# Prompt tiles that store their mixed rows to DRAM, and a second phase that does out-projection, norm and router for all tiles with the decode chain between its steps

## The reference

```python
xn = rms_norm(x, norm1); proj = xn @ w_in          # q 512 | k 128 | v 128 | z 512 | xBC 1024 | dt 8
q, k = rope(rms_norm(q)), rope(rms_norm(k))
attn = sliding_window_attention(q, k, v, window=128, sinks)      # sample rows: 128 cached keys and values
ssm  = ssd(conv4(xBC), dt, a, chunk=128) ; g = ssm * silu(z) ; ssm = group_rms_norm(g) * ssm_norm
h = x + concat(attn, ssm) @ w_out
t = rms_norm(h, norm2)                             # router: best of 4 groups, best 2 of its 8 experts
y = h + sum_k gate_k * (silu(t @ w_gate[e_k]) * (t @ w_up[e_k])) @ w_down[e_k]      # 32 experts, FF 128
```

## Time and profile before

| | |
|---|---|
| median of 3 runs | 940.5 us (936.82 to 942.17) |
| profiled execution, first to last instruction | 939.0 us |
| TensorE busy | 823.0 us, 88% |
| VectorE busy | 479.8 us, 51% |
| ScalarE busy | 258.4 us, 28% |
| GpSimd busy | 147.8 us, 16% |
| mean granted TensorE clock | 0.923 |
| moved by DMA | 119.43 MB |

### The profile page before, as it was taken

How to read it: one execution, slowest core, us unless ns; L and a number is a source line. 1 busy time by engine, 2 the same in 40 slices (tenths; PEclk the granted TensorE clock), 3 DMA queues, 4 the chain that set the end, 5 groups by cost and what they waited for, 6 DMA issues and landing times.

```text
span 939.0 us, 13161 instructions
## 1 busy us (share of the span) xinstructions
PE 823.0 (88%) x4478; PEld 583.9 (62%) x4478; DVE 479.8 (51%) x1357; ACT 258.4 (28%) x607; POOL 147.8 (16%) x238
## 2 busy tenths in 40 slices
PE   5999999999999999999999995298599999999910
PEld 2877577676686695785786532243388887777800
DVE  1766585675765766766765731175412222222236
ACT  1251351431531621522513412141022222221200
POOL 0011001010101110110110110023133333333200
PEclk9999999999999999999999997557689999999965
DMA  7940100100100101001001001564589998887268
GB/s 254 313 119 2 68 1 2 69 1 1 69 0 23 46 0 59 10 0 69 0 0 50 8 18 62 164 253 134 184 276 332 338 331 292 315 292 289 81 227 335
DMA packets 56354, 119.43 MB, mean 127 GB/s; under 512 B 15198, under 2 KB 27246, under 8 KB 56286
## 3 DMA queue, kind: packets, MB, share of 16 engines
q1 hardware_dynamic: 43590, 89.31, 27.9%
q0 software_dynamic: 9216, 16.93, 4.9%
q10 hardware_dynamic: 3504, 12.68, 3.5%
...
## 4 chain that ended last, share of the span: by engine, by line
issue 46%; PE 21%; DMA 14%; SPq 7%; POOL 5%; DVE 3%; ACT 1%; POOLq 1%; DVEq 1%; ACTq 0%
DMA w_arena<-in_w_down 8%; PE bank L1689 8%; PE bank L1695 4%; SPq L408 3%; SPq L404 3%; POOL rstd L1273 3%; DMA w_arena<-y_dram 3%; PE bank L1405 3%; PE bank L1418 2%; DMA w_arena<-in_w_in 1%; DVE cv L891 1%; POOL xde L1304 1%; POOL xd L1301 1%; DMA pT<-v_new 1%; POOLq L1272 1%
## 5 line engine op out<-in xcount | busy, mean ns | idle before, releaser
L1418 PE MATMUL bank<-w_arena,xT 128*128 128x512 f32 (+3 forms) x464 | 174.8, 533 | 3.2 <-DMA w_arena<-in_w_in 3.2
L1418 PEld LDWEIGHTS bank<-w_arena,xT 128*128 128x128 f32 (+1 forms) x464 | 79.4, 175 | 88.7 <-issue 83.1
L1689 PEld LDWEIGHTS bank<-w_arena 128*128 128x128 f32 x992 | 116.9, 195 | 26.0 <-issue 20.6
L1689 PE MATMUL bank<-w_arena 128*128 128x128 f32 x992 | 119.1, 279 | 7.4 <-DMA w_arena<-in_w_down 6.4
L1435 PE MATMUL bank<-xT,w_arena 128*128 128x128 f32 x1024 | 116.8, 275 | 0.0
L1435 PEld LDWEIGHTS bank<-xT,w_arena 128*128 128x128 f32 x1024 | 116.1, 192 | 0.5
L1271 POOL TENSOR_TENSOR stat<-stat,eps 128x1 f32<-128x1 f32 (+4 forms) x35 | 6.8, 193 | 447.1 <-ACT junk L557 160.0
L1208 DVE TENSOR_TENSOR w_arena<-w_arena,bank 128x128 f32<-128x128 f32 x32 | 9.2, 288 | 112.8 <-ACT w_arena L692 112.8
L1695 PE MATMUL bank<-w_arena 128*128 128x512 f32 x124 | 60.4, 609 | 0.7 <-DVE w_arena L1208 0.7
L1449 PE MATMUL bank<-w_out_sb,aT 128*128 128x512 f32 x128 | 57.7, 593 | 0.0
L1449 PE MATMUL bank<-w_out_sb,gT 128*128 128x512 f32 x128 | 57.5, 592 | 0.0
...
## 6 DMA issues: line engine op xcount, KB each, us to landing
...
```

Source lines behind the costliest of these rows:

```text
L1418: ins = pe.matmul(out, xT[:, k, 0:n], w_in[:, k, cols], start=k == 0, stop=k == KC - 1)
L1689: ins = pe.matmul(out[:, a * P:(a + 1) * P], gu[:, a, k, :], xgT[w % 2][:, k, :], start=k == 0, stop=k == KC - 1)
```

## The change

The tile loop now ends at the SSD rows. Attention output and normed SSD rows of a tile share one buffer, `mix`, which the SP queue stores to `mix_dram` (`spill`). A second phase of nine steps follows, in the order tiles 0 to 6, sample rows, tile 7 (`ORDER`). Step i loads `mix` and x of its tile back (`load_back`, two buffers), multiplies in two halves of 512 columns (`pe_out(i, 0)`, `pe_out(i, 1)`), and between the halves and behind them come the transposes, ranks and router of the steps before and the pieces of the decode chain. `dve_front` is cut in three and its first two parts move ahead of the SSD gate; ACT's softplus moves with them. The new key and value row are issued ahead of the cache copies. The expert phase and the last part are as before, but the program asks for `dynamic_dma_scratch_size=8192`.

```diff
--- before.py
+++ after.py
...
+        mix_dram = nc.dram_tensor("mix_dram", (TILES, P, D), F32, kind="Internal").ap()
...
-        aT = sb("aT", [P, REP, P])
+        mix = sb("mix", [P, KC, P])
+        aT, gT = mix[:, 0:REP, :], mix[:, REP:KC, :]
+        mix_back = [sb(f"mix_back{u}", [P, KC, P]) for u in range(2)]
...
+        ORDER = (*range(TILES - 1), TILES, TILES - 1)
...
+        def back(i):
+            return x[(i + 1) % 2]
+
+        def back_landed(i):
+            return 32 * (i // 2) + (32 if ORDER[i] < TILES else 16)
...
+            def spill(tile, dst):
+                now(sp, "at gt", tile)
+                sp.dma_start(dst, mix[:, :, :].rearrange("p k n -> p (k n)")).then_inc(mix_out, 16)
...
                     sp.wait_ge(first_in, 32)
-                    sp.wait_ge(S["td"], t0 + (u + CREDIT + 1))
+                    sp.wait_ge(S["qkr"], t0 + (u + CREDIT + 1))
...
+                    sp.wait_ge(S["xn"], t0 + (u + CREDIT + 1))
                     sp.dma_start(x[u][:, :], flat_x[bass.ds(t0 * P + (u + 2) * P, P), :]).then_inc(x_in[u], 16)
...
+                    spill(t0 + u, mix_dram[bass.ds(t0 + u, 1)].rearrange("a p n -> (a p) n"))
...
+            def load_back(i):
+                tile = ORDER[i]
+                if tile < TILES:
+                    sp.dma_start(mix_back[i % 2][:, :, :].rearrange("p k n -> p (k n)"), mix_dram[tile]).then_inc(back_in[i % 2], 16)
+                    sp.dma_start(back(i)[:, :], flat_x[tile * P:(tile + 1) * P, :]).then_inc(back_in[i % 2], 16)
+                else:
+                    sp.dma_start(back(i)[0:DEC, :], I["x_sample"].rearrange("b s d -> (b s) d")).then_inc(back_in[i % 2], 16)
+
+            def load_next_back(i):
+                now(sp, "wob td", i - 2)
+                sp.wait_ge(h_out[i % 2], 16 * (i // 2))
+                load_back(i)
...
+            now(sp, "xn", TILES - 1)
+            sp.wait_ge(mix_out, 16 * TILES)
+            load_back(0)
+            now(sp, "xn", TILES)
+            load_back(1)
...
             sp.dma_start(keys[0:P - 1, :, :], ck[1:P]).then_inc(cache_in, 16)
             sp.dma_start(vals[0:P - 1, :, :], cw[1:P]).then_inc(cache_in, 16)
+            now(sp, "qkr qkv", TILES)
+            new_k = qkr[0:DEC, 8:10, :].rearrange("p a b -> p (a b)")
+            new_v = v_new[0:DEC, :]
+            sp.dma_start(keys[P - 1:P, :, :], new_k).then_inc(cache_in, 16)
+            sp.dma_start(vals[P - 1:P, :, :], new_v).then_inc(cache_in, 16)
+            spill(TILES - 1, mix_dram[TILES - 1])
             for name in ("k", "v"):
...
+            def store_state(b):
+                sp.wait_ge(T["hup"], b + 1)
+                sp.dma_start(O["ssm_sample"][0, b].rearrange("(c l) p n -> (l p) c n", l=2), st_h[:, b]).then_inc(outs, 16)
...
+            load_next_back(2)
             for w in range(RING):
                 for one in expert_weights(w, wgu[w], wd[w]):
                     one.then_inc(e_w[w], 16)
-
+            load_next_back(3)
+            load_next_back(4)
+            store_state(0)
+            store_state(1)
+            load_next_back(5)
+            store_state(2)
+            store_state(3)
+            load_next_back(6)
             sp.wait_ge(T["att"], 7)
             for one in load_gate_up(NE - 2, late_wgu[0]):
                 one.then_inc(e_w_late, 16)
+            store_state(4)
+            store_state(5)
+            load_next_back(7)
...
-                if not first:
-                    act_router(act, tile - 1, P)
...
+                act_softplus(act, tile + 1, n_next)
                 now(act, "pv", tile)
-                last(act, "wom", tile)
+                act.wait_ge(mix_out, spilled)
...
-                act_softplus(act, tile + 1, n_next)
                 act_raw(act, tile + 1, n_next, 1)
-                act.drain()
-                act_residual(act, tile, u, P, dram_rows)
-                act_store_t(act, tile, u, P, dram_rows)
                 act_z(act, tile + 1, n_next)
-                act_turned_t(act, tile, P)
...
+            act_residual(act, 0)
+            act_store_t(act, 0)
             act.wait_ge(T["kT"], 1)
...
+            act_turned_t(act, 0, P)
...
+            for i in range(2, TILES + 1):
+                act_residual(act, i)
+                act_store_t(act, i)
+                act_router(act, i - 1, width(ORDER[i - 1]))
+                if i == 2:
+                    act_state(0)
+                    act_state(1)
+                act_turned_t(act, i, width(ORDER[i]))
+                if i == 3:
+                    act_state(2)
+                    act_state(3)
+                if i == 4:
+                    act_state(4)
+                    act_state(5)
+                if i == 5:
+                    act_state(6)
+                    act_state(7)
+            act_router(act, TILES, P)
...
+        def dve_residual(dve, i, c):
+            n, h = width(ORDER[i]), back(i)[0:width(ORDER[i]), 512 * c:512 * c + 512]
+            now(dve, ("woa", "wob")[c], i)
+            if c == 0:
+                dve.wait_ge(back_in[i % 2], back_landed(i))
+            dve.tensor_tensor(h, h, bank[4 - c][0:n, :], ALU.add).then_inc(S[("hra", "hres")[c]], 1)
...
+                dve_front_dt(dve, tile + 1, n_next)
...
+                dve_front_a(dve, tile + 1, n_next)
...
+
+                if n_next == DEC:
+                    dve.wait_ge(kv_out, 32)
+                dve_front_qk(dve, tile + 1, 1 - u, n_next, x_need)
                 now(dve, "ytm", tile)
-                last(dve, "wom", tile)
+                dve.wait_ge(mix_out, spilled)
                 dve.tensor_tensor(gT[:, :, :], bank[3][:, :].rearrange("p (c n) -> p c n", c=4),
                                   ssm_norm[:, :].unsqueeze(2).to_broadcast([P, 4, P]), ALU.mult).then_inc(S["gt"], 1)
-
-                if n_next == DEC:
-                    dve.wait_ge(kv_out, 32)
-                dve_front(dve, tile + 1, 1 - u, n_next, x_need)
                 if n_next == P:
                     dve_conv(tile + 1, 0)
-                dve_residual(dve, tile, u, P)
-                if n_next == P:
                     dve_keys(tile + 1)
-                if slot is None:
-                    dve.wait_ge(loaded, n_loaded[0])
-                dve_norm2(dve, tile, u, P, t_free)
-                if n_next == P:
                     dve_conv(tile + 1, 1)
...
+            dve.wait_ge(loaded, n_loaded[0])
+            for i in range(TILES + 1):
+                n = width(ORDER[i])
+                dve_residual(dve, i, 0)
+                if i >= 2:
+                    dve_rank_read(dve, i - 2, P)
+                    dve_rank(dve, i - 2, P, slot_of(i - 2))
+                if i == 1:
+                    dve_queries()
+                    dve_state_conv()
+                if i == 2:
+                    dve_scores_top()
+                    dve_head_scales()
+                if i == 3:
+                    dve_attention()
+                    dve.wait_ge(state_in, 16 * DEC)
+                    dve_state(0)
+                    dve_state(1)
...
+                dve_residual(dve, i, 1)
+                if i == 1:
+                    dve_keys_turned()
+                if i == 2:
+                    dve_rows_bc()
...
+                dve_norm2(dve, i)
+                if i >= 1:
+                    dve_router(dve, i - 1, width(ORDER[i - 1]), slot_of(i - 1))
...
+                pool_qk(tile + 1, n_next)
...
+            for i in range(TILES + 1):
+                if 3 <= i <= 6:
+                    pool_state(2 * i - 6)
+                    pool_state(2 * i - 5)
+                pool_h(i, width(ORDER[i]))
...
+        def pe_out(pe, i, c):
+            u = i % 2
+            if c == 0:
+                pe.wait_ge(back_in[u], back_landed(i))
+            last(pe, ("hra", "hres")[c], i)
+            for k in range(KC):
+                ins = pe.matmul(bank[4 - c][:, :], mix_back[u][:, k, :], w_out[:, k, 512 * c:512 * c + 512], start=k == 0, stop=k == KC - 1)
+            ins.then_inc(S[("woa", "wob")[c]], 1)
...
-                now(pe, "at gt std", tile)
-                pe_out(pe, tile, P)
                 if n_next == P:
                     pe_keys(nxt)
                 pe_z(pe, nxt, n_next)
-                if n_next == P:
-                    now(pe, "qkc", nxt)
-                pe_turn_t(pe, tile, P)
-
-            pe_tile(0, P, first=True)
...
+            now(pe, "at gt", TILES - 1)
+            for i in range(TILES + 1):
+                if ORDER[i] < TILES:
+                    pe_out(pe, i, 0)
+                else:
+                    last(pe, "hra hres", i)
+                    pe_out_half(pe, DEC, 0, (0, 1))
+                if i >= 1:
+                    pe_turn_t(pe, i - 1, width(ORDER[i - 1]))
+                if i >= 2:
+                    pe_rank(pe, i - 2, P)
+                if i == 1:
+                    pe_keys_turned()
+                if i == 2:
+                    pe_rows_bc()
```

(47 more changed lines are left out.)

578 lines of the change are left out of this document (278 added, 300 removed).

## The result

The median of the changed kernel is 945.8 us (940.9 to 949.4, 19 runs), of the kernel before 940.0 us (936.8 to 944.1, 19 runs): a ratio of 1.0061, 95% interval 1.0046 to 1.0076. It is slower by 0.6%, where 923, 1.9% faster than the 940.5 then known, was forecast; 945.8 lies outside the range of 908 to 937. The profiled execution has a span of 942.6 us, against the forecast's 921.3.

What follows compares the result with a forecast made beforehand. TensorE, busy 88%, was taken as the bound. Phase 2's start at 445.4, plus 191.5 and a 20.4 tail, ended the slots at 657.3, 17.7 earlier; span 921.3, plus 1.5, gave 923 us, range 908 to 937.

Steps and rivals of the forecast that it cites:

- Phase 2 starts at 445.4: End of the tile loop: tiles start at 49.1, then 47.3 for tile 0, 298.7 for tiles 1 to 6, 50.3 for tile 7.
- The wait for keys, 15.2: Second phase, before the cached keys' transposes: TensorE waits 15.2 us for the cache loads, bounds 10 and 22.
- The rest up to the last out-projection, "at the upper clock": Second phase: out-projections 123.7 us, transposes, router and ranks 23.6, decode matmuls and small items 19.6, new waits 7.0.
- the reload: Second phase, step 2: its load lands 54 to 56 us after the phase starts, needed at 53.8; costed at 1 us.
- The tail, 20.4: From the last out-projection to the slot table's last matmul: 20.4 us, bounds 15 and 24, against 15.4 before.
- The expert phase unchanged: From the slots' end to the kernel's end: 264 us as before, so the span falls by the 17.7 us gained earlier.
- rival B: Second phase: small waits and narrow matmuls bring the 0.50 clock back, costing 10 to 19 us, 933 to 942; chance 10%.
- A: Second phase, steps 2 and 3: TensorE waits for reloads of `mix_back`, costing 5 to 12 us, 928 to 935; chance 10%.
- C: Second phase: the key wait vanishes as cache loads finish in time, 15.2 + 2.4 us less, 905; chance 5%.
- D: Tile loop: VectorE's chain becomes the bound; at 4 us over 28.8 in seven tiles, 951; chance 9%.
- E: Expert phase: the smaller descriptor scratch delays POOL's gathers; a tenth more is 26 us, 949; chance 3%.
- The claim on one DMA engine: Cache loads: 127 partitions run on one of sixteen DMA engines; with all sixteen, the key stall would be gone.

Runs made afterwards that it cites:

- rows_early: The changed kernel with ScalarE's square and scaling of the next tile's rows moved to the end of the tile before, ahead of z: 921.0 us.
- scratch_before: The kernel before with only the changed kernel's smaller descriptor scratch (`dynamic_dma_scratch_size=8192`): 939.1 us, ratio 1.000.
- fill_waits: The changed kernel with four extra 128x512 matmuls in each of steps 4 and 5, ahead of the state broadcasts TensorE waits for: 945.7 us.
- full_rows: The changed kernel with cut cache loads, early normed rows and second-phase waits removed (893.4 us), plus state broadcasts over 128 partitions instead of 8: 886.0 us.
- full_rows_waits: The changed kernel with cut cache loads (920.3 us), plus state broadcasts over 128 partitions, the second phase's waits left in: 917.5 us.
- best: The changed kernel with cut cache loads, early normed rows, phase waits removed, 128-partition broadcasts, sample rows last, two row buffers exchanged back: 881.6 us.
- split_before: The kernel before with each of the two 127-partition cache loads cut into 112 and 15 partitions: 911.2 us, ratio 0.969.

## Why the prediction was wrong

The span was forecast as 921.3 and came as 942.6, 21.3 us more. By the prediction's own steps:

- *Phase 2 starts at 445.4*: it was 449.5, 4.1 more. 1.5 is the prologue of this execution (first scores at 50.55, not 49.09), 3.1 tiles 1 to 6 (301.8, not 298.7), tile 7 gave 0.6 back. The wait for normed rows was sized nearly right, 1.9 to 2.0 against 1.7, 1.6 us over the six tiles. The rest is that the sum kept "the two or three short dips": with that wait in each tile there are four, where before had two. rows_early, which takes out 9.8 us of waits there, shortens the six tiles by 15.4.
- *The wait for keys, 15.2*: right, 14.24, and it ended 37.6 after the start, not 38.4.
- *The rest up to the last out-projection, "at the upper clock"*: this is the step that failed. From the key transposes on it took 169.6 us, not 153.1. Of these 16.5 us, 9.8 are the clock: 2.4 were allowed for one recovery, and it cost 0.9 at the key transposes and 11.3 in the eight halves. 5.3 are waits: 12.3 instead of 7.0. The two of 2.3 in steps 4 and 5 were right (2.11 each). That of 2.4 before the sample's second half did not come; 0.46 us stand before the first half and 0.37 before the means ahead of it. Not foreseen were 4.12 us at the transposes of the state rows, where VectorE turned score maxima first. And 3.13 us went to the x rows of step 2, the reload that was costed "at 1 us, inside the rounding": it landed at 55.1 us after the start, inside the 54 to 56 of the prediction, but TensorE asked at 52.0 and not at 53.8. The last 1.4 is spread over narrow matmuls.
- *The tail, 20.4*: right, 20.7. *The expert phase unchanged*: 265.2 against 264.0; scratch_before says that the scratch isn't the cause, which stays open.

What came is rival B, which had a tenth of the chance, joined by a part of A. Its cost of the clock, 9.8 us where the prediction gives 10 to 19, was sized about right; the 945.8 lies 3.8 us beyond its 933 to 942, since 5.3 us of waits and 4.1 us up to the start of phase 2 came on top. The prediction even had the row that spoke for it: 33.8 of 37.6 us busy was not enough to hold the clock. It was outweighed by the argument that the phase is dense on average. The runs show that the average does not decide: fill_waits (a wait filled, the half behind it at 7.13), full_rows (partitions filled, four halves back to 7.03 to 7.13) and full_rows_waits (waits kept, the three halves behind them slow). What they do not show is why the same stretch without a wait brings a slow half in one execution and not in another.

One reading of the prediction was off without harm to its sum: the slices in which the clock of before falls are 25 to 30, 563 to 704 us, not 23 to 27 and 520 to 640. Rivals C, D and E did not happen. The claim on one DMA engine held in what follows from it: cut to 112 and 15 partitions, the loads cost TensorE no wait. Which engines carried them was not read from a trace.

What the change is worth by itself is also measured: with the loads cut in both kernels, 9.0 us slower. What it makes possible is worth more. The x buffer that it frees early lets the rows be normed a stretch ahead, and with the waits and the weak stretches gone, best is 29.6 us under split_before and 60.7 us under the kernel before in its own comparison. Whether an order as good exists without the second phase was not tried.
